# A two-block network on one core: modulation products as VectorE dot products in the MLPs, and w_out in two halves

## What is computed

```python
for l in range(DEPTH):                      # first block
    mx = split(silu(c) @ w_ada[l] + b_ada[l], 6)            # and mc from c_ctx
    hx = modulate(rmsnorm(x, g_pre_mix[l]), mx[0], mx[1])
    out_x, out_c = token_mixers(hx, hc, w_in[l], w_out[l], ...)
    x = x + mx[2] * rmsnorm(out_x, g_post_mix[l])
    hx = modulate(rmsnorm(x, g_pre_mlp[l]), mx[3], mx[4])
    x = x + mx[5] * rmsnorm(sq_relu_mlp(hx, w_mlp1[l], w_mlp2[l]), g_post_mlp[l])
    ...                                     # the same for ctx in layer 0
# token_mixers: concatenate([ym, yf, yv]) @ w_out
#   ym: mLSTM heads (channels 0-511), yf: Fourier mix (512-767), yv: gated convolution (768-1023)
for l in range(DEPTH):                      # second block
    shift, scale, gate = split(silu(c_2) @ ada_w_2[l] + ada_b_2[l], 3)
    ...
```

## Time and profile before

| | |
|---|---|
| median of the three runs | 3289.57 us (3286.33 to 3298.46) |
| span of the profiled execution | 3296.2 us |
| TensorE busy | 3061.9 us, 93% |
| VectorE, ScalarE, GpSimd busy | 1369.8, 1076.6, 1119.3 us |
| mean granted TensorE clock | 0.941 |
| chain that ended last, by engine | PE 82%, DVE 11%, ACT 3%, issue 2% |
| DMA | 275.49 MB, mean 84 GB/s |

### The profile page before, as it was taken

One profiled execution on the slowest core, in us unless ns is written; L12 is line 12 of the kernel. 1 busy time (PEld: TensorE's weight loads), 2 busy tenths in 40 slices (PEclk: granted clock), 3 DMA queues, 4 the chain that ended last, 5 costly groups with the idle time before them and its releaser, 6 DMA issues.

```text
span 3296.2 us, 42947 instructions
## 1 busy us (share of the span) xinstructions
PE 3061.9 (93%) x16748; PEld 2466.0 (75%) x16748; DVE 1369.8 (42%) x2601; ACT 1076.6 (33%) x1995; POOL 1119.3 (34%) x862
## 2 busy tenths in 40 slices
PE   7998879999999988978999999999889999998898
PEld 4687658888888866856788876777678767776786
DVE  4683432512122158242531125644482255434822
ACT  3223432323222242243333332233433322334332
POOL 1121104133233422203344442342355523332555
PEclk9999869899999979988899989999999899999999
DMA  5232252121111112333222222121112222121121
GB/s 205 90 141 84 100 195 77 45 64 63 60 65 64 65 59 78 112 113 109 100 96 96 91 84 77 64 69 67 58 58 77 85 71 70 65 65 64 58 77 64
DMA packets 77720, 275.49 MB, mean 84 GB/s; under 512 B 8512, under 2 KB 10304, under 8 KB 77392
## 3 DMA queue, kind: packets, MB, share of 16 engines
q1 hardware_dynamic: 75824, 268.91, 24.0%
q10 hardware_dynamic: 1696, 3.84, 0.3%
HBM read 270.62 MB, written 2.10 MB: 83 GB/s over the span
## 4 chain that ended last, share of the span: by engine, by line
PE 82%; DVE 11%; ACT 3%; issue 2%; POOL 1%; DMA 1%; SPq 0%; DVEq 0%; ACTq 0%; POOLq 0%
PE pb L1054 19%; PE pb L1056 18%; PE pb L1055 18%; PE pb L1165 2%; PE pb L997 2%; PE pb L1076 2%; PE pb L1078 2%; PE pb L1077 2%; PE pb L1093 1%; DVE AR L1717 1%; PE pb L1094 1%; PE pb L1095 1%; PE pb L1123 1%; PE pb L1173 1%; PE pb L1299 1%
## 5 line engine op out<-in xcount | busy, mean ns | idle before, releaser
L2622 POOL TENSOR_TENSOR RGR<-RG,WHI 128x512 fp32r<-128x512 f32 x708 | 933.9, 1328 | 1746.3 <-ACT WHI L2210 1745.5
L2210 ACT ACTIVATE WHI<-RG 128x512 fp32r<-128x512 f32 x708 | 436.9, 624 | 711.4 <-PE pb L1056 600.5
L1054 PE MATMUL pb<-HI,WHI 128*128 128x512 f32 (+1 forms) x880 | 374.5, 426 | 10.5 <-DVE LO L1645 4.9
L1056 PE MATMUL pb<-LO,WHI 128*128 128x512 f32 (+1 forms) x880 | 351.3, 399 | 0.0
L1055 PE MATMUL pb<-HI,RGR 128*128 128x512 f32 (+1 forms) x880 | 350.7, 398 | 0.0
L1054 PE MATMUL pb<-HR,WHI 128*128 128x512 f32 (+1 forms) x768 | 276.8, 360 | 8.1 <-DVE HR L1645 5.6
L1056 PE MATMUL pb<-HR,WHI 128*128 128x512 f32 (+1 forms) x768 | 276.9, 361 | 0.0
L1055 PE MATMUL pb<-HR,RGR 128*128 128x512 f32 (+1 forms) x768 | 276.6, 360 | 0.0
L1056 PE MATMUL pb<-HIDR,WHI 128*128 128x512 f32 (+1 forms) x768 | 274.7, 358 | 0.0
L1055 PE MATMUL pb<-HIDR,RGR 128*128 128x512 f32 (+1 forms) x768 | 274.2, 357 | 0.0
L1054 PE MATMUL pb<-HIDR,WHI 128*128 128x512 f32 (+1 forms) x768 | 273.3, 356 | 0.0
(11 more groups left out here) (407 smaller groups left out, 5665.1 us busy)
## 6 DMA issues: line engine op xcount, KB each, us to landing
RG<-in_W_dram SPq DMA_DIRECT2D x504, 512.0 KB, 3.5
XCX<-in_xT_dram ACTq DMA_DIRECT2D x4, 512.0 KB, 12.2
out_dram<-XCX SPq DMA_DIRECT2D x8, 256.0 KB, 2.1
CS<-in_CST_dram ACTq DMA_DIRECT2D x1, 1027.0 KB, 4.8
XCC<-in_ctxT_dram SPq DMA_DIRECT2D x4, 256.0 KB, 13.9
CS<-in_CST_dram SPq DMA_DIRECT2D x1, 523.0 KB, 4.7
RG<-in_W_dram SPq DMA_DIRECT2D x2, 256.0 KB, 2.9
RG<-in_W_dram SPq DMA_DIRECT2D x2, 128.0 KB, 2.6
```

Of the source, the lines that this page charges most:

```text
L1054: e.matmul(out, hi[:, k, :], xh, start=k == order[0], stop=False)
L1056: i = e.matmul(out, hi[:, k, :], xl, start=False, stop=k == order[7])
L2210: e.activation(WHI[:, u % 2, h * n:h * n + n], RG[:, s % RING, h * n:h * n + n], ACT.Copy).then_inc(*up("weightsA", (u, h)))
L2622: e.tensor_tensor(RGR[:, s % RING, sl], RG[:, s % RING, sl], WHI[:, u % 2, sl].bitcast(F32), SUB).then_inc(*up("weightsG", (u, h)))
```

## The change

1. 24 modulation products of layer 0's mixer (columns 40 to 47 of layer 0 and 0 to 39 of layer 1, in units of 128) and the 18 of layer 1's mixer leave TensorE. They become *columns*: the host lays the weight slab out transposed (128 output channels on the partitions, 1024 inputs along them), silu(c) is copied to all partitions (`SPREAD`), and VectorE multiplies and sums with one SCALAR_TENSOR_TENSOR with an accumulated output per conditioning vector, two in the first block and one in the second. They run in the two MLPs, one at most per `period` of 8 and 5 modelled us. `offsets` adds the biases at the end, and the gains that need them move there.
2. w_out becomes two pieces of kind `H` with four inner tiles each: `half` on tiles 4 to 7, woven between the mLSTM's later steps with two banks, copied to OUT, and `out` on tiles 0 to 3 at the old place, added to OUT.
3. The periods of the mLSTM's steps now come from the length of og and of the half.

```diff
+    def column(self, i, j, name, l):
+        n = self.piece("column", [self.slab(name + ":T", l, 0, 8, j * 128, 128)], [], [], i=i, j=j, how="column")
+        self.last["column", i] = n
+        self.loaded.append(n)
+    def columns(self, period, *what):
+        self.period, self.credit = period, 0.0
+        for i, js, name, l in what:
+            self.sums += [(i, j, name, l) for j in js]
+    def next_column(self):
+        if self.loaded and (len(self.loaded) > 1 or not self.sums):
+            self.step("column", self.loaded.pop(0))
+        if self.sums:
+            self.column(*self.sums.pop(0))
...
         if self.credit >= self.period and self.fills:
             self.credit = 0.0
             self.ada(*self.fills.pop(0))
+        elif self.credit >= self.period and (self.sums or self.loaded):
+            self.credit = 0.0
+            self.next_column()
...
-                    out.append({**new, "k0": k0, "nk": 4 if kind == "N" else 8})
+                    out.append({**new, "k0": k0, "nk": 4 if kind in "NH" else 8})
...
+                elif kind == "H":
+                    self.run(p, [(0, 1), (2, 3)], gn / 512 * 2.8)
...
     if l == 0:
-        o.fill(8.5, (0, range(16, 48, 2), "w_ada", 0), (1, range(0, 40, 2), "w_ada", 1))
-    else:
-        o.fill(24.0, (2, range(0, 24, 2), "ada_w_2", 0), (3, range(8, 20, 2), "ada_w_2", 1))
+        o.fill(8.5, (0, range(16, 40, 2), "w_ada", 0))
...
-    stages = o.begin(mlstm_stages(l), 1.5)
+    stages = mlstm_stages(l)
+    before = [s[0] for s in stages].index("mO")
+    us = sum(gn for _, gn in go) / 512 * 22.4
+    stages = o.begin(stages, [us * 1.05 / before] * before + [(us + 7.0) / (len(stages) - before)] * (len(stages) - before))
     o.products([F(1536, 512, "og", "evacA", go)])
...
+    tag = f"o{l}a"
+    o.products([("H", "w_out", l, 4, 0, D, "half", "evacV", {"groups": go, "x": "MX", "tag": tag, "k0": 4})])
     o.rest(stages)
     o.filled()
-    o.step("gains", l, (1, 2, 3))
-    tag = f"o{l}a"
+    o.step("gains", l, (1, 2) if l == 0 else (1, 2, 3))
     o.turn = 3
-    o.products([("F", "w_out", l, 0, 0, D, "out", "evacV", {"groups": go, "x": "MX", "tag": tag, "ks": (4, 5, 6, 7, 0, 1, 2, 3)})], (0, 1, 2, 3))
+    o.products([("H", "w_out", l, 0, 0, D, "out", "evacV", {"groups": go, "x": "MX", "tag": tag, "k0": 0})], (0, 1, 2, 3))
+    o.step("spread", l)
     jobs = []
...
+    if l == 0:
+        o.columns(8.0, (0, range(40, 48), "w_ada", 0), (1, range(0, 40), "w_ada", 1))
+    else:
+        o.columns(5.0, (2, range(0, 24), "ada_w_2", 0), (3, range(8, 20), "ada_w_2", 1))
+    o.step("spreadSilu", l)
     o.products(jobs, (0, 1, 2, 3), 2)
     o.flush()
+    o.columned()
+    if l == 0:
+        o.step("offsets", 0, 40, 48)
+        o.step("offsets", 1, 0, 40)
+        o.step("gains", 0, (3,))
+    else:
+        o.step("offsets", 2, 0, 24)
+        o.step("offsets", 3, 8, 20)
     if tab:
...
+    SPREAD = [ar(31744, 2, 1024), OUTF[:, 0:4, 0:NC]]
+    PRODUCT = CS[:, IDR_AT - 1024:IDR_AT]
...
-                e.wait_ge(*at("matmuls", o.slabs[i - RING]["last"]))
+                older = o.slabs[i - RING]["last"]
+                e.wait_ge(*at("columnsV" if o.pieces[older]["kind"] == "column" else "matmuls", older))
...
+        def H(p, part, opening):
+            hi, lo = [half[:, :, p["j"]:p["j"] + 128] for half in halves(p)]
+            g0, gn = p["g0"], p["gn"]
+            out = PB[p["banks"][0]][:, 0:gn]
+            for k in part:
+                weights(p, k)
+                ready(p, p["k0"] + k, g0)
+                xh, xl = [x[:, g0:g0 + gn] for x in operands(p, p["k0"] + k)]
+                e.matmul(out, hi[:, k, :], xh, start=k == 0, stop=False)
+                e.matmul(out, lo[:, k, :], xh, start=False, stop=False)
+                i = e.matmul(out, hi[:, k, :], xl, start=False, stop=k == 3)
+                if k == 3:
+                    i.then_inc(*up("matmuls", p["n"]))
+                elif k == 1 and p["n"] == o.units[p["unit"]]["last"]:
+                    i.then_inc(*up("halvesP", p["unit"]))
...
+        def column(n):
+            p = o.pieces[n]
+            s, i = p["slabs"][0], p["i"]
+            w = RG[:, s % RING, :]
+            e.wait_ge(*at(f"slab{s % RING}", s))
+            e.wait_ge(*at("spreadA", min(i, 2)))
+            if i < 2:
+                if ("product", i) in seen:
+                    e.wait_ge(*now("columnsV"))
+                seen.add(("product", i))
+                e.scalar_tensor_tensor(out=PRODUCT, in0=w, scalar=1.0, in1=SPREAD[0][:, 0, :], op0=MUL, op1=MUL,
+                                       accum_out=MODS[i][:, p["j"], 0:1]).then_inc(*up("columnsV"))
+                e.wait_ge(*now("columnsV"))
+                e.scalar_tensor_tensor(out=w, in0=w, scalar=1.0, in1=SPREAD[0][:, 1, :], op0=MUL, op1=MUL,
+                                       accum_out=MODS[i][:, p["j"], 1:2]).then_inc(*up("columnsV", n))
+            else:
+                w4 = w.rearrange("p (a b) -> p a b", a=4)
+                e.scalar_tensor_tensor(out=w4, in0=w4, scalar=1.0, in1=SPREAD[1], op0=MUL, op1=MUL,
+                                       accum_out=MODS[i][:, p["j"], 0:1]).then_inc(*up("columnsV", n))
+        def offsets(i, j0, j1):
+            ns = 2 if i < 2 else 1
+            bias = vec(*(("b_ada", i) if i < 2 else ("ada_b_2", i - 2)))
+            mod = MODS[i][:, j0:j1, 0:ns]
+            e.wait_ge(*now("columnsV"))
+            e.tensor_tensor(mod, mod, bias[:, j0:j1].unsqueeze(2).to_broadcast([128, j1 - j0, ns]), ADD).then_inc(*up("columnsV", ("all", i, j0)))
...
+        def half(p, n):
+            e.wait_ge(*at("matmuls", n))
+            e.tensor_copy(cols(p, OUT[:, p["jj"], :]), bank(p)).then_inc(*up("evacV", n, ("half", p["l"], p["jj"], p["g0"])))
         def out(p, n):
+            d = cols(p, OUT[:, p["jj"], :])
             e.wait_ge(*at("matmuls", n))
-            e.tensor_copy(cols(p, OUT[:, p["jj"], :]), bank(p)).then_inc(*up("evacV", n))
+            e.wait_ge(*at("evacV", ("half", p["l"], p["jj"], p["g0"])))
+            e.tensor_tensor(d, d, bank(p), ADD).then_inc(*up("evacV", n))
...
+        def spread(l):
+            e.wait_ge(*at("matmuls", o.last["out", l, "evacV", None]))
+            if l == 0:
+                e.wait_ge(*at("normG", ("heads lo", 0, CHUNKS[1][5])))
+                e.dma_start(fl(SPREAD[0]), dram["VEC"][:, NVEC:NVEC + 2 * D]).then_inc(*up("spread", l, by=16))
+            else:
+                e.dma_start(SPREAD[1], dram["VEC"][:, NVEC + 2 * D:NVEC + 3 * D].rearrange("p (a b) -> p a b", a=4)).then_inc(*up("spread", l, by=16))
+        def spreadSilu(l):
+            e.wait_ge(*at("spread", l))
+            if l == 0:
+                e.activation(SPREAD[0], SPREAD[0], ACT.Silu).then_inc(*up("spreadA", 0, 1))
+            else:
+                e.activation(SPREAD[1], SPREAD[1], ACT.Silu).then_inc(*up("spreadA", 2))
...
+        if name.endswith(":T"):
+            W[i] = inputs[name[:-2]][l][:, c0:c0 + n].T
+            continue
```

More of the change, by code:

```diff
@@ L219, in ada, with columned @@
         self.soon.append(n)
+    def column(self, i, j, name, l):
[11 more added lines that the diff above has]
+            self.column(*self.sums.pop(0))
+    def columned(self):
+        while self.sums or self.loaded:
+            self.next_column()
     def hold(self, i, j, name, l):
@@ L295, in tasks @@
         for kind, name, l, k0, cols, n, how, by, more in jobs:
-            per = 256 if kind in "TN" else 128
+            per = 256 if kind in "TNH" else 128
             for t, j0 in enumerate(range(0, n, per)):
@@ L358, in products @@
                 continue
-            while made < len(tasks) and (made <= i or not any(x["kind"] in "FTN" for x in tasks[i + 1:made])):
+            while made < len(tasks) and (made <= i or not any(x["kind"] in "FTNH" for x in tasks[i + 1:made])):
                 x = tasks[made]
@@ L398, in cost @@
         p = self.pieces[what[1]]
-        if p["kind"] == "F":
+        if p["kind"] in "FH":
             return len(what[2]) * p["gn"] / 512 * 0.7
@@ L418, in place @@
                 first.setdefault(self.pieces[what[1]].get("unit"), i)
+            if what[0] == "column":
+                taken[what[1]] = i
             if what[0] == "ev":
@@ L976, in halves @@
             s, u = p["slabs"][0] % RING, p["unit"]
-            nk = 4 if p["kind"] == "N" else p.get("nk", 8)
+            nk = 4 if p["kind"] in "NH" else p.get("nk", 8)
             n = o.units[u]["n"]
@@ L1598, in gains @@
         def gains(l, which):
-            e.wait_ge(*at("evacV", o.last["ada", l, 0 if which == (0,) else 2]))
+            if which == (3,):
+                e.wait_ge(*at("columnsV", ("all", 0, 40)))
+            else:
+                if which == (0,) and l:
+                    e.wait_ge(*at("columnsV", ("all", 1, 0)))
+                else:
+                    e.wait_ge(*at("evacV", o.last["ada", l, 0 if which == (0,) else 2]))
```

(14 more changed lines are left out.)

15 lines of the change are left out of this document (10 added, 5 removed).

## The result

The changed kernel takes **3342.36 us** in the median of four runs (3338.16 to 3347.51), the kernel before 3287.95 beside it: a ratio of **1.0147** (95% interval 1.0128 to 1.0166). It is slower by 54 us; the forecast was 3185, in a range of 3125 to 3240. The profiled execution has a span of 3336.4 us against 3296.2.

The account below looks back on a forecast made before the run. It took TensorE's own work, plus its waits and low-clock stretches, to bound the kernel. Terms -112 + 16 - 16 + 5 + 2 = -105 us from the median of 3289.57 gave 3185 us, range 3125 to 3240.

Parts of the forecast that it names:

- part 1: Both mixers: 42 of 72 modulation products leave TensorE, with the waits tied to them; 112 us gained.
- rival 1: Mixers: mLSTM's chain alone sets the pace; of the products only 16.3 + 4.7 + 11.0 gained; 3201 us, worse 3233; chance 0.22.
- part 2: Mixers: half of w_out fills gaps between mLSTM steps, by itself zero; waits +16 us, clock -16 us.
- The waits in the mixers: TensorE's waits not for modulation products: from 16 to 24 us in layer 0, 24 to 32 in layer 1; +16 us.
- The clock: mLSTM stretches: half of a possible 17.6 and 13.7 us regained, -16 us; layer 0's clock above 0.8.
- The column's length: VectorE in the MLPs: one column instruction takes 1.5 to 2 us.
- The spread vectors' DMA and Silu: Ahead of the MLPs: two more DMAs and Silus on ScalarE cost +2 us, from 0 to 4.
- Part 3's cover of 5.1 and 10.7 us: MLPs: time left over for columns before a weight slab's use, 5.1 us in layer 1, 10.7 in layer 0; priced +5 us.
- a wait for RGR in the MLPs: Sign in the MLPs: TensorE at 99% or more expected; a wait for RGR or WHI would prove part 3's cover wrong.
- Rival 3: MLPs: columns over 5.1 us starve them, loses from about 6 us, 3300 or more at 7 us; chance 0.04.

Follow-up runs that it names:

- Experiment 1: Changed kernel with w_out undivided behind the mLSTM and the steps' old period of 1.5 us: 3364.0 us, ratio 1.0216 to the kernel before.
- experiment 5: Changed kernel with a column put one piece after its slab is asked for, not two, still behind the evacuation: 3196.59 us, ratio 0.9697 to the kernel before.
- 11: Changed kernel with a column one piece after its slab is asked for, not two, measured again: 3202.34 us, ratio 0.9722 to the kernel before.
- experiment 4: Changed kernel with the column ahead of the evacuation on VectorE instead of behind it: 3207.2 us, ratio 0.9734 to the kernel before.

## Why the prediction was wrong

- **Parts 1 and 2, the mixers: right in the sum, in part by luck.** -112 + 16 - 16 + 2 = -110 was forecast, -106.9 came; -70.5 in layer 0 is what its terms give, -36.4 in layer 1 falls 3 to 4 short. The shares were not as written. Experiment 1 shows 79 us for the removal, where part 1 had 112 and rival 1 had 32, and 28 for the halves, which part 2 counted as worth nothing by themselves. So of the 80 us of products inside the mLSTM's chain some 47 came back with nothing in their place, and the halves, standing in the gaps, brought most of the rest.
- **Where it came in layer 0.** The og product ended at 349.8 before and at 338.2 after: 11.6 us earlier, where 4.7 were forecast; in it, from 284 on TensorE waited 8.1 us before (5.8 of them L1054's for ScalarE's AR) and waits 2.4 now. From there to w_out's second half it took 123.1 us (338.2 to 461.3), where 145.5 were before and about 106 were forecast. The two misses go against each other.
- **The waits in the mixers: near in the sum, not in the parts.** Forecast 24 and 32 us. The waits of TensorE from the end of og to w_out's end (338 to 495) sum to 30.4, those in 1380 to 1533 to 31.6. Of the latter 9.0 are L1204's for ScalarE's squares of the layer norm, 1.8 before (L1138), which no term had, and 2.8 are for the split, where 7 were forecast. Of before, the prediction's 16 us take in one row of L997 (1.7 us, for AR); without it it is 14.6. The largest, and the new one of layer 0 (forecast 7, with GpSimd's 1.4 it is 5.1):

```profile
PE pb L1407 <- DVE AR L2033: 7.5, 2, 4.5
...
PE pb L1159 <- ACT MXH L2608: 3.7, 1, 3.7
...
PE pb L1159 <- POOL MXL L2769: 1.4, 2, 0.9
```

- **The clock: about right.** From 338 to 461 it was 0.85; over 0.8 was forecast. Of the slices 4 to 6 that the prediction names as low, slice 4 reads 9 (5 and 6 read 8 and 6, and slice 8 reads 8); nothing rests on that.
- **The column's length: near.** Forecast 1.5 to 2 us; 1.22 us alone, plus 0.08 to read the accumulator, and 2.2 when it starts while GpSimd's instruction runs.
- **The spread vectors' DMA and Silu: nothing.** From w_out's end to MLP 0's first matmul it is 35 us after and 36 before.
- **Part 3's cover of 5.1 and 10.7 us: this step failed.** The sum priced it at 5 us, and the MLPs lost 145.1. It gave a weight slab the two tasks since the reading of its slot. But SyncE issues in order, and the column's slab ahead of it needs the slot of a column that had been put off by two pieces: of three pieces only one was left. And "0.7 us of evacuation" was that of w_mlp2 (L1760). A piece of w_mlp1 has the relu, the square, the rounding and the low part, some 3.4 us (747.92 to 751.3), and the relu stands on ScalarE behind the split that waits for the very transfer in question. The sum 0.7 + 1.5 + 3.5 + 0.6 + 1.3 held every link of a line; the links closed into a ring, which has to fit within one piece. With the trace's durations: 0.3 for SyncE, 4.5 to landing, 0.5, 0.6 relu, 1.5 square, 0.6, 0.6 and 1.3 for the column are the 10 us against 5.6. Ahead of the run, 3.5 to landing, 0.6 for the split, four evacuation instructions at the 0.7 of L1760 and 1.5 for the column would have given 8.4, too long for 5.6, and 9.9 with the second column of layer 0, too long for 8.4. The prediction's own sign of this, a wait for RGR in the MLPs, came true.
- **Rival 3 had the right symptom and the wrong threshold.** It named starving MLPs but asked for a column of 5.1 us or more, 6 to lose; with 1.22 us in MLP 1 they lost 2.0 us per column. Its 4% was the price of trusting the cover.
- **The sum without that step.** With the loop opened by one line (experiments 5 and 11) the medians are 99.8 and 86.7 us under the kernel before beside them; -105 was forecast, and 3125 to 3240 takes in both. The profile of experiment 5 is 105.3 us under that of before, but it is the fastest of its four executions.

## What to carry to other kernels

Before a reader is added to a ring of buffers that a queue refills in order, follow the slot round: freeing reader, refill, every engine queue that the refilled data must pass, back to the next freeing reader, and compare that sum with the time of the number of pieces it may span. A slot's distance in the ring says little when the reader is put off by some pieces; the distance from the reader to the next issue counts. Here moving the reader one place earlier gave all of the loss back, while cutting its work to a sixteenth gave half (70 of 145 us).

## What the runs showed of the hardware

- SCALAR_TENSOR_TENSOR on VectorE with two float32 SBUF sources, 128x1024, with an accumulated output takes 1219 ns alone, no more per element than a TENSOR_TENSOR (0.69 us for 128x512). The Trainium skill (Vector Engine (DVE) Microarchitecture Reference, Points that are easy to get wrong) has half throughput for it; these durations do not bear it out.
- The doubled durations have another cause. Column groups of the changed kernel and of experiment 4, 600 to 1000:

```profile
L1659 DVE SCALAR_TENSOR_TENSOR RG<-RG,AR 128x1024 f32<-128x1024 f32 x41 | 82.7, 2016 | 1.4
...
L1663 DVE SCALAR_TENSOR_TENSOR RG<-RG,AR 128x1024 f32<-128x1024 f32 x46 | 56.3, 1225 | 1.6
```

  The same instruction, at another phase to GpSimd's, is free of it. What decides is which of the two starts first. In experiment 5 each of the 48 first instructions of a pair started ahead of GpSimd's and took 1.2 us with GpSimd's beside it, which took 1.9 to 2.4 (1.29 alone); each of the 48 second ones started while GpSimd's ran and took 2.2. Its groups, 600 to 1000:

```profile
L1659 DVE SCALAR_TENSOR_TENSOR RG<-RG,AR 128x1024 f32<-128x1024 f32 x45 | 98.5, 2189 | 1.6
L1656 DVE SCALAR_TENSOR_TENSOR CS<-RG,AR 128x1024 f32<-128x1024 f32 x45 | 54.8, 1219 | 0.0
```

  That GpSimd's two-source instruction and VectorE's hold each other up (64 elements in 1.19 us) agrees with the Trainium skill (SBUF — State Buffer, Who interferes with whom). It cost nothing where no loop passed through it: MLP 0 of experiment 5 took 611.3 us.
- Of two slabs issued one right behind the other, as the loop makes it, the second lands later: in 600 to 1000 of the changed kernel 3.6 us in the median for the first of 40 such pairs and 4.5 for the second (4.4 over all 81 slabs), against 3.5 in the earlier trace rows and 3.55 in experiment 5, whose 92 slabs of the same window hold no such pair.
